# A decoder trunk on one Trainium2 core: the first modulation scale computed ahead of its shift, and six column blocks instead of five kept open in the first stage

## The reference

```python
c_act = jax.nn.silu(c)
mod = c_act @ ada_w[l] + ada_b[l]                      # 6 parts of 1024
sh_m, sc_m, g_m, sh_f, sc_f, g_f = jnp.split(mod, N_MOD, axis=-1)
h = rms_norm(x, norm_mix_g[l]) * (1 + sc_m) + sh_m
u = h @ w_in                                           # 1024 -> 3072
b_g, c_g, xv = jnp.split(u, 3, axis=-1)
z = c_g * xv                                           # then conv3, * b_g, @ w_out
x = x + g_m * y
```

## Time and profile before

| what | value |
|---|---|
| median of three runs | 1161.05 us |
| the profiled execution | 1160.05 us |
| its span (first to last instruction) | 1158.3 us |
| PE busy, share of the span | 1152.1 us, 99% |
| DVE busy, ACT busy | 75%, 47% |
| granted TensorE clock, all of it | 1.00 |

### The profile page before, as it was taken

The page is one execution under the profiler, slowest core; times in us unless marked ns, Lnnn a source line. Parts: engine busy times, 40 slices in busy tenths (PEclk is TensorE's granted clock), DMA queues, the critical chain, the costliest instruction groups (busy, mean ns, idle before and its releaser), DMA issues.

```text
span 1158.3 us, 16333 instructions
## 1 busy us (share of the span) xinstructions
PE 1152.1 (99%) x5839; PEld 967.7 (84%) x5839; DVE 866.7 (75%) x1191; ACT 543.4 (47%) x876; POOL 25.3 (2%) x37
## 2 busy tenths in 40 slices
PE   8999999999999999999999999999999999999999
PEld 6788889988888888888978888889988888888887
DVE  4666988975675675555889988897887778779694
ACT  5322333531331341333677887775665445445521
POOL 2000000000000000200020000000000000000000
PEclk9999999999999999999999999999999999999999
DMA  9977655476666666333255554464133323332311
GB/s 296 293 220 229 200 178 184 128 232 189 197 192 192 196 190 191 93 92 91 74 128 142 131 132 127 110 164 146 40 103 114 109 81 103 108 119 82 108 56 73
DMA packets 207324, 168.89 MB, mean 146 GB/s; under 512 B 5684, under 2 KB 180188, under 8 KB 207260
## 3 DMA queue, kind: packets, MB, share of 16 engines
q1 hardware_dynamic: 207068, 167.92, 49.2%
q10 hardware_dynamic: 160, 0.06, 0.0%
q0 software_dynamic: 32, 0.07, 0.0%
HBM read 153.24 MB, written 2.10 MB: 134 GB/s over the span
## 4 chain that ended last, share of the span: by engine, by line
PE 95%; DVE 2%; DMA 1%; ACT 1%; SPq 0%; issue 0%; DVEq 0%
PE bank L788 24%; PE bank L789 24%; PE bank L790 24%; PE bank L1102 4%; PE bank L1103 4%; PE bank L1104 4%; PE bank L1279 2%; PE bank L1261 2%; PE bank L1251 1%; PE bank L1252 1%; PE bank L970 1%; PE bank L971 1%; PE bank L973 1%; PE bank L927 1%; DMA ada_first<-in_ada_w 1%; DVE h_lo L2005 0%
## 5 line engine op out<-in xcount | busy, mean ns | idle before, releaser
L788 PE MATMUL bank<-h_hi,w_hi 128*128 128x512 f32 (+1 forms) x848 | 318.8, 376 | 0.3 <-DVE h_lo L2005 0.3
L790 PE MATMUL bank<-h_hi,w_lo 128*128 128x512 f32 (+1 forms) x848 | 316.5, 373 | 0.0
L789 PE MATMUL bank<-h_lo,w_hi 128*128 128x512 f32 (+1 forms) x848 | 316.4, 373 | 0.0
L1418 ACT ACTIVATE w_hi<-raw 128x1024 fp32r<-128x1024 f32 x149 | 156.3, 1054 | 154.4 <-DMA raw<-in_mlp_w 116.4
L1951 DVE TENSOR_TENSOR w_lo<-raw,w_hi 128x1024 fp32r<-128x1024 f32 x149 | 181.4, 1221 | 33.4 <-ACT w_hi L1418 32.5
L788 PEld LDWEIGHTS bank<-h_hi,w_hi 128*128 128x128 f32 x848 | 159.7, 188 | 29.1 <-DVE h_lo L2005 0.8
L790 PEld LDWEIGHTS bank<-h_hi,w_lo 128*128 128x128 f32 x848 | 159.7, 188 | 28.4
L789 PEld LDWEIGHTS bank<-h_lo,w_hi 128*128 128x128 f32 x848 | 159.7, 188 | 27.6 <-issue 0.2
L788 PE MATMUL bank<-g_hi,w_hi 128*128 128x512 f32 (+1 forms) x416 | 154.8, 372 | 0.0
L790 PE MATMUL bank<-g_hi,w_lo 128*128 128x512 f32 (+1 forms) x416 | 153.5, 369 | 0.0
L789 PE MATMUL bank<-g_lo,w_hi 128*128 128x512 f32 (+1 forms) x416 | 153.4, 369 | 0.0
(11 more groups left out here) (293 smaller groups left out, 1684.1 us busy)
## 6 DMA issues: line engine op xcount, KB each, us to landing
raw<-in_mlp_w SPq DMA_DIRECT2D x96, 512.0 KB, 4.0
ada_raw<-in_ada_w SPq DMA_DIRECT2D x40, 1024.0 KB, 5.6
w_raw<-in_mlp_w SPq DMA_DIRECT2D x32, 512.0 KB, 3.4
raw<-in_sc_w_in SPq DMA_DIRECT2D x18, 512.0 KB, 4.1
raw<-in_w_kv SPq DMA_DIRECT2D x16, 512.0 KB, 3.9
ada_first<-in_ada_w SPq DMA_DIRECT2D x24, 256.0 KB, 5.8
raw<-in_q_w SPq DMA_DIRECT2D x8, 512.0 KB, 4.8
keys<-qk SPq DMA_DIRECT2D x16, 256.0 KB, 3.1
```

Of the source, the lines that this page charges most:

```text
L788: mm(out[:, cols], weights_hi, hi[:, k, cols], start=(k == 0), stop=False)
L789: mm(out[:, cols], weights_hi, lo[:, k, cols], start=False, stop=False)
L790: return mm(out[:, cols], weights_lo, hi[:, k, cols], start=False, stop=(k == KT - 1))
L1418: go(w_hi[:, jj, :, :], raw[:, jj, :, :], ACT.Copy).then_inc(hi_ok, 1)
```

## The change

It has two parts.

**The first unit in two halves.** SP loads the scale's columns of unit 0 (both halves of k) ahead of the shift's. PE multiplies the scale's eight strips of 128 columns (`strips_0(1)`), sums them (`sum_0(1)`), and DVE adds the bias, makes the gain and scales tile 0; the shift's strips, copy and sum follow (`strips_0(0)`, `take_0(0)`, `sum_0(0)`, `add_0(0)`), and ACT waits for the shift before it makes `h_hi`. From here the counts of `ada_strip`, `ada_taken`, `ada_turned` and `ada_red` are one unit higher (`SUMS`).

**Six open blocks.** Block 5 joins the first stage, in bank 7, with the `beside` buffers. Its weights come for two k at a time, behind those of block 4. Behind the stage are blocks 6 (slot 1) and 7 (slot 2, in two loads of half a block), then block 8 as before. The load of block 8 no longer waits for the end of the stage. The splits of blocks 6 to 8 stand at other places of ACT and DVE.

```diff
-FIRST_BLOCKS = GROUP + 1
-FIRST_BANK = [0, 1, 2, 3, 5]
+SUMS = UNITS + 1
+FIRST_BLOCKS = GROUP + 2
+FIRST_BANK = [0, 1, 2, 3, 5, 7]
-X_TAKEN = [1, 2, 3, KT - 1, KT - 2]
-SOON, LATE_BLOCKS = (0, 1, 2, 4), (3,)
+X_TAKEN = [1, 2, 3, KT - 1, KT - 2, KT]
+SOON = (0, 1, 2)
...
+            def ada_unit_0():
+                for n in (1, 0):
+                    for half in range(2):
+                        k = slice(half * STRIPS, (half + 1) * STRIPS)
+                        sp.dma_start(ada_first[:, 0, k, n, :], ada_rows[:, k, n * D:n * D + P]).then_inc(ada_in[0][1 - n], 16)
...
+                    sp.dma_start(beside_raw[:, 0, k:k + 2, :], first_w[:, k:k + 2, c0 + P:c0 + 2 * P]
+                                 ).then_inc(spare_in[k // 2] if k // 2 < KT // 2 - 1 else beside_in, 16)
...
             sp.wait_ge(first_used, 2)
-            load_block(1, c_g(GROUP + 1))
+            load_block(1, c_g(GROUP + 2))
             sp.wait_ge(ms_ok, TT)
             ada_pair(0, 0, 2, 0)
             sp.wait_ge(first_used, 3)
-            load_block(2, c_g(GROUP + 2))
+            sp.dma_start(raw[:, 2, 0:STRIPS, :], c_g(GROUP + 3)[:, 0:STRIPS, :]).then_inc(raw_in[2], 16)
             ada_pair(1, 0, 2, 1)
             sp.wait_ge(hi_ok, KT // 2)
-            sp.dma_start(beside_raw[:, 0, :, :], c_g(GROUP + 3)).then_inc(raw_in[3], 16)
+            sp.dma_start(raw[:, 2, STRIPS:, :], c_g(GROUP + 3)[:, STRIPS:, :]).then_inc(raw_in[3], 16)
             x_v = columns(sc_w_in[0], 2 * D)
-            sp.wait_ge(pe_done, FIRST_BLOCKS)
             load_block(0, x_v(0))
...
-                    sp.wait_ge(pe_done, KT + n - 3)
+                    sp.wait_ge(pe_done, KT + n - (2 if n < 3 else 3))
                     load_block(s, x_v(n))
...
-            unit_strips(0, (0,))
             x_turn(4)
-            unit_strips(0, (1,))
+            strips_0(1)
             inv_turn()
-            unit_sum(0)
+            sum_0(1)
             x_turn(5)
+            strips_0(0)
             x_turn(6)
+            sum_0(0)
             x_turn(7)
             opening_high(0)
             opening_high(1)
-            opening_late()
+            opening_late((4, 3))
+            opening_low(range(0, 3))
             unit_strips(1)
-            opening_low(range(0, 2))
+            opening_late((5,))
+            opening_low((3, 4))
             unit_sum(1)
-            opening_low(range(2, FIRST_BLOCKS))
+            opening_low((5,))
             opening_rest()
...
+                    act.wait_ge(ada_red, 2)
                     act.wait_ge(hs_half, 1)
...
-                if j == 1:
-                    split_beside()
-                if j >= FIRST_BLOCKS:
+                if j == 3:
+                    split_seventh()
+                if j > GROUP:
                     split(g, jj + 3)
...
                 if j == 1:
-                    split_beside()
-                if j >= FIRST_BLOCKS:
+                    split_late(2)
+                if j == GROUP:
+                    split(2, 0)
+                if j > GROUP + 1:
                     split(g, jj + 3)
                 ada_step(g, jj, j, 2)
```

More of the change, by code:

```diff
@@ L913, in inv_turn, with strips_0, sum_0 @@
                 v.then_inc(inv_turned, 1)
+            def strips_0(n):
+                pe.wait_ge(ada_in[0][1 - n], 32)
+                if n == 0:
+                    pe.wait_ge(ada_red, 1)
+                for k in range(KT):
+                    i = k % STRIPS
+                    strip = mm(bank[6][32 * i:32 * i + 32, 0:P], c_wide[:, k, :], ada_first[:, 0, k, n, :],
+                               start=(k < STRIPS), stop=(k >= STRIPS), skip_group_check=True)
+                    if k >= STRIPS:
+                        strip.then_inc(ada_strip, 1)
+            def sum_0(n):
+                pe.wait_ge(ada_taken, 2 - n)
+                mm(bank[6][:, 0:1], ada_acc[:, n * D:n * D + P], ones[:, 0:1], start=True, stop=True,
+                   skip_group_check=True).then_inc(ada_turned, 1)
             def unit_strips(e, halves=(0, 1)):
-                if e:
-                    pe.wait_ge(ada_red, e)
+                pe.wait_ge(ada_red, e + 1)
                 for half in halves:
@@ L934, in unit_sum @@
                 units = 2 if e in PAIRED else 1
-                pe.wait_ge(ada_taken, e + units)
+                pe.wait_ge(ada_taken, e + units + 1)
                 for n in range(2):
@@ L991, in opening_high, with opening_late @@
                        stop=False, skip_group_check=True)
-            def opening_late():
-                for b in LATE_BLOCKS:
+            def opening_late(blocks):
+                for b in blocks:
                     pe.wait_ge(x_ok, X_TAKEN[b])
@@ L1047, in _ @@
             pe.wait_ge(x_ok, KT)
-            turn(bank[7][:, 0:ROWS], rows_a[:], ident[0:ROWS, 0:ROWS]).then_inc(cols_pe, 1)
-            for jj in range(FIRST_BLOCKS - GROUP, GROUP - 1):
-                dense(1, jj, h_hi, h_lo)
-            pe.wait_ge(bank_free, GROUP)
-            part_of(KT - 1, 0, bank[GROUP - 1], h_hi, h_lo, range(KT), weights=(beside_hi, beside_lo)).then_inc(pe_done, 1)
+            turn(bank[4][:, 0:ROWS], rows_a[:], ident[0:ROWS, 0:ROWS]).then_inc(cols_pe, 1)
+            for b in range(FIRST_BLOCKS, KT):
+                pe.wait_ge(bank_free, b - 3)
+                part_of(b, b - FIRST_BLOCKS + 1, bank[b - GROUP], h_hi, h_lo, range(KT)).then_inc(pe_done, 1)
             layer(2, 3 * KT // GROUP - 2, h_hi, h_lo, None)
@@ L2175, in _ @@
             stt(out=inv, in0=half_y2, scalar=1.5, in1=y, op0=ALU.add, op1=ALU.mult).then_inc(inv_ok, 1)
+            take_0(1)
+            add_0(1)
+            gain(0, 0, 1, R_MIX, 1, (0, 1))
             for k in range(KT):
-                if k in PAIRED or k < PAIRED[0]:
+                if k and (k in PAIRED or k < PAIRED[0]):
                     unit_take(k)
@@ L2183, in _, with split_late @@
                 split_first_spare(k)
-            split(1, 1)
-            split(1, 2)
+            def split_late(s):
+                dve.wait_ge(hi_ok, FIRST_BLOCKS + s)
+                tt(w_lo[:, s, :, :], raw[:, s, :, :], w_hi[:, s, :, :], ALU.subtract).then_inc(lo_ok, 1)
+            split_late(1)
             dve.wait_ge(cols_pe, 3)
-            nc.vector.tensor_copy(cols[:, R_MLP:ROWS], bank[7][:, R_MLP:ROWS]).then_inc(cols_ok, 1)
+            nc.vector.tensor_copy(cols[:, R_MLP:ROWS], bank[4][:, R_MLP:ROWS]).then_inc(cols_ok, 1)
             dve.wait_ge(cols_ok, 3)
```

71 lines of the change are left out of this document (49 added, 22 removed).

## The result

The changed kernel takes 1162.31 us (median of 22 runs, 1161.34 to 1164.96), the kernel before 1160.07 us beside it (22 runs, 1159.72 to 1161.6). The ratio is 1.0019, with a 95% interval from 1.0013 to 1.0025: slower by 2.2 us. Two single executions of the experiments, of 3423 us (experiment 6) and 2788 us (experiment 9), are left out of every figure.

A forecast was written before the change was run, and what follows sets the result against it. PE was taken to bound the kernel, busy for 1152.1 of 1158.3 us. An opening gain of 0.6 us and a 1.8 us wait at block 9 made +1.2 us on 1161.05, so 1162.25 us; range 1160.2 to 1163.6.

The forecast's parts named there:

- the wait at block 9: Behind the first stage: weights ready 18.3 us after PE's turn of the columns, due after 16.46; PE waits 1.8 us.
- The rival without a wait: At block 9: DVE or the loads run sooner and PE does not wait; 1160.45 us, or 1159.7; chance 0.17.
- its form with 0.6 us: At block 9: pricing a DMA at about 2 us plus bytes at 436 GB/s gives a 0.6 us wait, median 1161.05.
- the gain of 0.6 us in the opening: At tile 2's start: 28.75 us against 29.38 to compare with, between ends of 0 and 1.35 us.
- The chain of scale and shift: In the opening: scale handled first, shift after; PE's first product moves from 16.38 to about 15.5, 0.9 us earlier.
- the claim that unit 3's last load is the one that holds PE: In the opening: two beside loads ahead make it land at 28.23 instead of 27.37, with only 0.1 us of slack.
- each beside load adding 0.43 us: On SP's packed queue in the opening: each new 128 KB load delays all behind it by 0.43 us.
- The rival "the opening gives nothing": In the opening: ACT waits for the shift, tiles 1 to 3 for later loads; 1162.85 us; chance 0.18.
- A wait of 1.8 us is nowhere in the rows, and I add nothing.: At block 9's wait: a clock loss is possible, but no row shows one, so it is costed at nothing.
- The block-10 rival: From opening to block 10 the load queue sets the pace: waits of 2.5 us, no opening gain, 1163.55 us; chance 0.12.
- the 5.4 us that the rival set as its mark: At block 10: the rival holds if its low part starts over 5.4 us behind block 9's.
- The sum: Whole kernel: -0.6 us in the opening and +1.8 at block 9 give +1.2 us, median 1162.25.

The follow-up runs named there:

- experiment 6: Changed kernel with the loads of blocks 9 and 10 moved ahead in SP's order, block 9's before the pairs; 1160.36 us, ratio 1.0001 to the kernel before.
- experiment 9: Kernel before with PE's ten 128x256 warm-up matmuls replaced by twenty of 128x128; 1160.17 us, ratio 0.9998.
- experiment 3: Changed kernel with unit 0 loaded and multiplied whole as before, so six open blocks alone; 1162.57 us, ratio 1.0020 to the kernel before.
- experiment 2: Kernel before with unit 0 in two halves, scale first, and five open blocks as before; 1160.40 us, ratio 1.0003.
- experiment 7: Experiment 6 with two blocks of tile 1 ahead of unit 2's strips and one of tile 2 ahead of unit 3's; 1160.28 us, ratio 1.0000.
- experiment 1: Changed kernel with block 9's load issued ahead of the two pairs of the modulation steps; 1164.06 us, ratio 1.0028 to the kernel before.
- experiment 8: Experiment 2 with one block of tile 1 and of tile 2 ahead of the strips of units 2 and 3; 1160.66 us, ratio 1.0003.
- experiment 5: Changed kernel with block 9's load held back until modulation step 5 is done; 1166.02 us, ratio 1.0048 to the kernel before.
- experiment 10: Experiment 2 with five warm-up matmuls of PE instead of ten; 1161.34 us, ratio 1.0004 to the kernel before.

## Why the prediction was right, and where it was not

**Right: the wait at block 9.** It was forecast in its place, with its chain and its releaser, and experiment 6 shows that it is the whole loss: without it the ratio is 1.0001 instead of 1.0019. In size 1.8 us was 2.05. The steps were: low part ready at turn + 18.3 (measured 18.6; the load took 7.2 us for 6.8 and was issued 9.13 behind the turn for 9.1), due at turn + 16.46 (PE arrived at 78.11, turn + 16.6).

**Right: what the step does not need.** The halves of unit 0 play no part in it (experiment 3: ratio 1.0020), since the wait counts from the turn, and what comes sooner in front of the turn moves both. The rival without a wait is out with the 2.05 us, and so is its form with 0.6 us, which priced the loads at less than the 7.2 us that block 9's took.

**Wrong: "I take this value, since the data sets it", the gain of 0.6 us in the opening.** It gave nothing (-0.1 by the turn). The chain of scale and shift was read rightly: the first product stands 4.36 us behind the first strips (10.65 to 15.01) where it stood 5.33 behind them (11.05 to 16.38), a gain of 0.97 for the forecast 0.9. That it came at 15.01 and not at 15.5 is the earlier start of the strips. The failing part is the claim that unit 3's last load is the one that holds PE, each beside load adding 0.43 us. Unit 3 landed at 28.21, as forecast (28.23), and nobody waited for it: PE had lost its lead at unit 2, whose last load landed 1.6 us later than before, where 0.43 was expected. Experiment 2 shows that the beside loads are not even needed for this, and experiment 7 that behind the loads stands the next thing, the chain that makes tile 1's `h`. That 0.6 us was booked on the first limit found, and there were three close together. The rival "the opening gives nothing" is the half that came true; with the wait its loss was 1.8 us, and measured were 2.2.

**Missing: the clock.** "A wait of 1.8 us is nowhere in the rows, and I add nothing." For 19 of 22 executions this held, and for the median too. In the other three the clock fell; in the one of them that was profiled, this cost another 1.7 us on top of 2.05 us of idle time. The sentence was honest on what the rows show; the range should have had it as a term of its own. One reading beside it is wrong: PE's longest wait of the opening before is not the 0.80 us but one of 1.2 us for `c_wide`, ahead of its first matmul. No term of the sum hangs on it.

**The block-10 rival.** The second low part came 84.55 - 78.88 = 5.67 us behind the first, over the 5.4 us that the rival set as its mark. The profile shows no wait for it, because half clock had put PE back. At full clock PE would have come to block 10 at 80.16 + 5.42 = 85.58, and the low part was ready at 85.78: a wait of 0.2 us by this estimate, where the rival had 0.7. Its mechanism is real. As soon as block 9 was helped (experiment 1), PE waited ahead of block 10 for 2.5 us.

**The sum** had -0.6 + 1.8 = +1.2, and is +0.1 + 2.05, or +2.2 us, with the wait as profiled. So it was short by 0.7 us in the opening and by 0.25 us in the wait. The remaining 1.0 us between the forecast time and the forecast difference is the base: three runs of the kernel before happened to lie high. That the two errors cancel is the luck.

No version here is faster than the kernel before. The best, experiments 6 and 7, can't be told from it.

## What to carry to other kernels

When work is moved ahead of a point on which a queue of loads hangs, count for every block behind that point when it is due and when it is ready, both from the point itself; the difference is the slack, and one block less between them takes it away at once. If a load in an ordered queue is late, look first when the next ones are ready: where they are no earlier, helping the first alone hands the wait to the next one behind the same gate, so move the queue's order for all of them, or none. And a start that comes earlier by a microsecond is worth that only if the next two or three deliveries (loads, then the chain made from them) come earlier as well.

## What the runs showed of the hardware

- **A short wait can halve TensorE's clock, and not every time.** With a wait of PE of 1.4 us in the profile (experiment 3) 1 of 11 executions has a mean clock below 1.00; with 2.05 us 3 of 22; with 2.5 us 3 of 6 and 5 of 6; with 2.6 us in the opening 7 of 10; with 3.4 us 4 of 4. The kernel before and experiments 2 and 6 to 9, whose longest waits are 1.2 us, have none. The length of the wait is known for the profiled execution of each alone. In the profiles of the changed kernel and of experiments 1, 5 and 10 the lower clock took 1.7 us of PE's work each time. It began 0.3 us ahead of PE's return (experiment 1, at 85.5) or 0.3 to 1.2 us behind it (80.4 in the changed kernel, 82.6 in experiment 5).
- **Much of a load's latency can be the queue ahead of it.** A 512 KB block took 3.7 us with no large load just ahead (experiment 1), 3.8 (experiment 5), 5.3 (block 10 in experiment 6, 2.1 us behind a pair) and 7.2 us right behind two loads of 1 MB.
- **An instruction fetch seems to show in a load's landing.** 16 KB on one DMA engine for about 1.2 us, and a load of 256 KB behind it that takes 6.8 to 7.2 us for 5.7 to 6.0, in six profiles of twelve each. None of them moved the fetch alone, so the cause is not shown.
- **The first 25 us forgive a lot.** PE's first product lay at 14.8 to 17.2 us in these kernels, and where no wait at block 9 or 10 followed the medians are 1160.1 to 1160.7 us, with one exception, experiment 10 (1161.34). Even there 1.6 us of the first product (16.88 for 15.28 in experiment 2) came to 0.1 us at the turn.
